# Two parts of a compression placed between the K/V groups of a sparse attention layer, and the turning of the Q rows beside the second part

## What is computed

```python
def nsa_shared_kv(s, w_kv, cmp_pe, cmp_w1, cmp_b1, cmp_w2, cmp_b2):
    kv = (s @ w_kv).reshape(B, S, 6, N_KV_HEADS, HEAD_DIM)
    k_c, v_c, k_s, v_s, k_w, v_w = kv[0], ..., kv[5]
    def compress(t, i):
        blocks = t[:, :, idx] + cmp_pe[i]              # 31 blocks of 32 tokens, stride 16
        flat = blocks.reshape(B, N_KV_HEADS, n_cmp, CMP_BLOCK * HEAD_DIM)
        hdn = jax.nn.gelu(flat @ cmp_w1[i] + cmp_b1[i])
        return hdn @ cmp_w2[i] + cmp_b2[i]
    kc = compress(k_c, 0)
    vc = compress(v_c, 1)
...
def nsa_mixer(u, ...):                                 # u = x * (1 + sc1) + sh1
    qg = u @ w_qg                                      # 1024 columns of Q, 48 of gates
```

## Time and profile before

| | |
|---|---|
| median of 3 runs | 1515.96 us (1513.84 to 1516.57) |
| the profiled execution | 1514.5 us, of which the span of the trace is 1512.7 us |
| PE busy | 1304.3 us (86%), mean granted clock 0.91 |
| DVE busy | 1077.6 us (71%) |
| ACT busy | 770.5 us (51%) |
| POOL busy | 304.5 us (20%) |

### The profile page before, as it was taken

One profiled execution on the slowest core, in us unless ns is written; L12 is line 12 of the kernel. 1 busy time (PEld: TensorE's weight loads), 2 busy tenths in 40 slices (PEclk: granted clock), 3 DMA queues, 4 the chain that ended last, 5 costly groups with the idle time before them and its releaser, 6 DMA issues.

```text
span 1512.7 us, 18392 instructions
## 1 busy us (share of the span) xinstructions
PE 1304.3 (86%) x6603; PEld 1013.3 (67%) x6603; DVE 1077.6 (71%) x1201; ACT 770.5 (51%) x998; POOL 304.5 (20%) x344
## 2 busy tenths in 40 slices
PE   1499988949999999869966899999984999999985
PEld 0277766847777777638964676775774777777772
DVE  5547773678888898565645566664276988988866
ACT  0323231327777777662422455657331777777760
POOL 3011111511000000107000445544441100000020
PEclk9699998759999999989957899999985999999998
DMA  8557765329999999924310333321531999999972
GB/s 311 217 186 243 266 223 225 119 84 367 391 388 382 393 392 386 375 97 143 114 55 6 112 98 99 112 79 62 198 135 54 367 405 389 391 387 390 392 289 91
DMA packets 107568, 356.07 MB, mean 235 GB/s; under 512 B 8034, under 2 KB 16446, under 8 KB 107470
## 3 DMA queue, kind: packets, MB, share of 16 engines
q1 hardware_dynamic: 82984, 269.52, 47.6%
q0 software_dynamic: 19952, 69.83, 13.3%
q10 hardware_dynamic: 4566, 15.84, 2.6%
HBM read 330.99 MB, written 25.21 MB: 235 GB/s over the span
## 4 chain that ended last, share of the span: by engine, by line
PE 51%; DVE 17%; issue 14%; ACT 9%; DMA 5%; POOL 2%; ACTq 1%; DVEq 0%; POOLq 0%; SPq 0%
PE bank L232 13%; PE bank L233 12%; PE bank L234 12%; ACT w_hi L1106 3%; DVE acc L360 3%; PE bank L1924 2%; PE bank L1942 2%; DMA xg<-scratch_u,tok 2%; PE bank L1912 1%; PE bank L1053 1%; DMA ada<-in_ada_w_dram 1%; DVE hh L1208 1%; POOL prob L2159 1%; PE bank L1147 1%; ACT xe_hi L1062 1%
## 5 line engine op out<-in xcount | busy, mean ns | idle before, releaser
L1112 DVE TENSOR_TENSOR w_lo<-raw,w_hi 128x2048 fp32r<-128x2048 f32 x189 | 436.9, 2317 | 69.8 <-ACT w_hi L1106 69.4
L1106 ACT ACTIVATE w_hi<-raw 128x2048 fp32r<-128x2048 f32 x189 | 362.5, 1919 | 84.6 <-PE bank L234 75.1
L232 PE MATMUL bank<-w_lo,xe_hi 128*128 128x512 f32 x512 | 211.9, 414 | 9.5 <-DVE xe_lo L1069 9.3
L234 PE MATMUL bank<-w_hi,xe_hi 128*128 128x512 f32 x512 | 203.9, 398 | 0.0
L233 PE MATMUL bank<-w_hi,xe_lo 128*128 128x512 f32 x512 | 203.6, 398 | 0.0
L227 DVE TENSOR_TENSOR w_lo<-raw,w_hi 128x2048 fp32r<-128x2048 f32 x37 | 85.7, 2321 | 144.8 <-ACT w_hi L222 144.7
L222 ACT ACTIVATE w_hi<-raw 128x2048 fp32r<-128x2048 f32 x37 | 70.5, 1909 | 160.0 <-PE bank L234 158.3
L232 PE MATMUL bank<-u_lo,w_hi 128*128 128x512 f32 x320 | 134.0, 419 | 17.8 <-DVE q L1826 9.3
L1042 POOL DMA_INDIRECT xg<-scratch_u,tok x32 | 38.2, 1194 | 551.2 <-DVE tok L1036 550.6
L233 PE MATMUL bank<-u_hi,w_lo 128*128 128x512 f32 x320 | 130.4, 407 | 0.0
L234 PE MATMUL bank<-u_hi,w_hi 128*128 128x512 f32 x320 | 130.3, 407 | 0.0
(11 more groups left out here) (289 smaller groups left out, 2378.5 us busy)
## 6 DMA issues: line engine op xcount, KB each, us to landing
raw<-in_w_gu_dram SPq DMA_DIRECT2D x128, 1024.0 KB, 8.2
raw<-in_w_down_dram SPq DMA_DIRECT2D x64, 1024.0 KB, 8.3
ada<-in_ada_w_dram POOLq DMA_DIRECT2D x64, 512.0 KB, 5.4
ada<-in_ada_w_dram SPq DMA_DIRECT2D x32, 512.0 KB, 3.8
scratch_y<-ye ACTq DMA_DIRECT2D x30, 512.0 KB, 7.5
raw<-in_conv_w_in_dram SPq DMA_DIRECT2D x12, 1024.0 KB, 9.7
raw<-in_w_kv_dram SPq DMA_DIRECT2D x6, 1024.0 KB, 8.4
rows<-scratch_mods POOLq DMA_DIRECT2D x10, 512.0 KB, 7.3
```

The source lines that it names most:

```text
L232: nc.tensor.matmul(o, lh, rl, start=start, stop=False)
L234: return nc.tensor.matmul(o, lh, rh, start=False, stop=stop)
L1106: nc.scalar.activation(w_hi[:, hslot, :], raw[:, slot, :], ACT.Copy).then_inc(hi_done, 1)
L1112: nc.vector.tensor_tensor(w_lo[:, slot, :], raw[:, slot, :], w_hi[:, hslot, :].bitcast(F32), ALU.subtract).then_inc(lo_done, 1)
```

## The change

The blocks are numbered in a new order, so that the two blocks of each part of the compression stand between K/V groups: group 0, group 1, part 0, group 2, part 1, Q. The loads, the splits and PE follow this order. The functions over all groups or both parts are cut into one per group or part, and the lists of `att_act` and `att_dve` are written out. PE turns the Q rows in four pieces: tile 0 and 1 before the first half of part 1, tile 2 and 3 between its halves. The first small product follows part 1, then the gates, then the second small product, then Q. The wait on `kc_made` moves behind the first half of the Q block. Group 2's K goes to banks 0 and 1, part 0 to banks 2 and 3, part 1 to banks 4 and 5, the turning to banks 2, 3, 6, 7. The buffers `w2`, `h1`, `kcf`, `vb2`, `wg` and `wg_hi` move from where the rows `u_hi` lie to the place of `kct`, which is free once `fl` is built; `wg_lo` takes the place of `wg`. POOL's small loads wait on `fl_made` and not on `blk_used`. No instruction of computation is added or left out.

```diff
+    B_KVG = [B_KV, B_KV + 2, B_KV + 6]
+    B_CMP = [B_KV + 4, B_KV + 8]
+    B_Q = B_KV + len(kv) + len(cmp1)
...
-        w2 = at("w2", [P, 2, HC, HD], F32, U0)
-        h1 = at("h1", [P, 2, HC, NC4], F32, U0 + KB)
-        kcf = at("kcf", [P, NC4], F32, U0 + 4 * KB)
-        wg = at("wg", [P, KD, 3 * NH], F32, S1 + 8 * KB)
+        w2 = at("w2", [P, 2, HC, HD], F32, S1)
+        h1 = at("h1", [P, 2, HC, NC4], F32, S1 + KB)
+        kcf = at("kcf", [P, NC4], F32, S1 + 3 * KB)
+        wg = at("wg", [P, KD, 3 * NH], F32, S1 + 4 * KB)
...
+        def compress_pe(pe, i, kh):
+            if kh == 0:
                 pe.wait_ge(fl_lo_made, i + 1)
                 if i == 0:
-                    pe.wait_ge(kv_v, 4)
-                    pe.wait_ge(kv_klo, 8)
...
+                    pe.wait_ge(kv_copy, 4)
+                else:
+                    pe.wait_ge(kv_v, 8)
...
+        def compress_out_pe(pe, i):
+
+            if i == 0:
+                pe.wait_ge(att_in, 16 * 3)
+                pe.wait_ge(*turn_q.lo.at(2 * TT))
+            pe.wait_ge(gelu_made, 2 * (i + 1))
...
         def q_pe(pe):
-            pe.wait_ge(kc_made, 3)
-            for i in range(TT):
-                turn_pe(pe, turn_q, us[:, i % 2, :], i)
...
+            pe.wait_ge(kv_klo, 8)
             for c_ in range(2):
                 if c_ == 1:
+                    pe.wait_ge(kc_made, 3)
...
         def att_pe(pe):
-            kv_pe(pe)
-            compress_pe(pe)
+            kv_pe(pe, 0)
+            kv_pe(pe, 1)
+            compress_pe(pe, 0, 0)
+            compress_pe(pe, 0, 1)
+            kv_pe(pe, 2)
+            pe.wait_ge(gelu_made, 2)
+            turn_pe(pe, turn_q, us[:, 0, :], 0)
+            pe.wait_ge(kv_v, 8)
+            turn_pe(pe, turn_q, us[:, 1, :], 1)
+            compress_pe(pe, 1, 0)
+            turn_pe(pe, turn_q, us[:, 0, :], 2)
+            turn_pe(pe, turn_q, us[:, 1, :], 3)
+            compress_pe(pe, 1, 1)
+            compress_out_pe(pe, 0)
+            gate_pe(pe)
+            compress_out_pe(pe, 1)
             q_pe(pe)
             attention_pe(pe)
...
-            pool.wait_ge(blk_used, B_CMP)
+            pool.wait_ge(fl_made, 1)
             pool.dma_start(w2[:], cmp_w2.rearrange("i (c p) d -> p i c d", p=P)).then_inc(att_in, 16)
...
-            pool.wait_ge(blk_used, B_Q)
+            pool.wait_ge(fl_made, 2)
             pool.dma_start(wg[:], w_qg[0].rearrange("(k p) n -> p k n", p=P)[:, :, D:D + 3 * NH]).then_inc(wg_in, 16)
...
         def att_sp(sp):
-            for b in range(3, 6):
-                load_block(sp, B_KV + b, kv[b])
+            load_block(sp, B_KVG[1] + 1, kv[3])
+            for kh in range(2):
+                load_block(sp, B_CMP[0] + kh, cmp1[kh])
...
```

More of the change, by code:

```diff
@@ L1578, in hybrid_trunk @@
         x_saved = sem("x_saved")
[L1580 to L1591, removed]
+        kbanks, vbanks = {1: (4, 5), 2: (0, 1)}, {1: (6, 7, 0, 1), 2: (4, 5, 6, 7)}
@@ L1600, in kv_pe @@
-                    if g:
-                        for i in range(TT):
[L1602 to L1669, removed]
@@ new lines, in kv_pe, with kct_act @@
+                            t = slice(i * P, (i + 1) * P)
+                            mm = mm3(bank[vbanks[g][i]][:, 0:2 * P], u_hi[:, k, t], u_lo[:, k, t],
+                                     wh[:, kk, 2 * P:4 * P], wl[:, kk, 2 * P:4 * P], start=(k == 0),
+                                     stop=(k == KD - 1))
+                        if kh == 1 and i < TT - 1:
+                            mm.then_inc(kv_mm, 1)
+                mm.then_inc(blk_used, 1)
+        def kct_act(act):
+            for m in range(4):
+                if m < 3:
+                    act.wait_ge(kv_mm, m + 1)
+                else:
+                    act.wait_ge(blk_used, B_KVG[0] + 2)
+                nc.scalar.activation(kct[:, m, :], bank[m][:], ACT.Copy).then_inc(kv_copy, 1)
@@ new lines, in k_hi_act @@
+        def k_hi_act(act, g):
+            for m in range(2):
+                act.wait_ge(kv_mm, 3 + 5 * (g - 1) + m + 1)
+                src = bank[kbanks[g][m]]
+                for h in range(2):
+                    part = slice(h * HD, (h + 1) * HD)
+                    for o in range(2):
+                        a = nc.scalar.activation(k2[o * HD:(o + 1) * HD, 2 * m + h, g - 1, :],
+                                                 src[part, :], ACT.Copy)
+                    a.then_inc(kv_khi, 1)
@@ L1699, in flat_lo_dve, with cmp_bank @@
             nc.vector.tensor_tensor(fl_lo[:], fl[:], fl_hi[:].bitcast(F32), ALU.subtract).then_inc(fl_lo_made, 1)
-        def compress_pe(pe):
-            for i in range(2):
+        def cmp_bank(i, hc):
+            return bank[(2, 4)[i] + hc]
+        def compress_pe(pe, i, kh):
+            if kh == 0:
                 pe.wait_ge(fl_lo_made, i + 1)
                 if i == 0:
-                    pe.wait_ge(kv_v, 4)
-                    pe.wait_ge(kv_klo, 8)
[L1707 to L1723, removed]
@@ new lines, in compress_pe @@
+                    pe.wait_ge(kv_copy, 4)
+                else:
+                    pe.wait_ge(kv_v, 8)
+            b = B_CMP[i] + kh
+            pe.wait_ge(lo_done, b + 1)
+            wh = w_hi[:, b % NSPLIT, :].rearrange("p (k n) -> p k n", n=HC * P)
+            wl = w_lo[:, b % NRAW, :].rearrange("p (k n) -> p k n", n=HC * P)
+            for kk in range(8):
+                k = 8 * kh + kk
+                for hc in range(HC):
+                    c_ = slice(hc * P, (hc + 1) * P)
+                    mm = mm3(cmp_bank(i, hc)[:, 0:NC4], wh[:, kk, c_], wl[:, kk, c_], fl_hi[:, k, :],
+                             fl_lo[:, k, :], start=(k == 0), stop=(k == 15))
@@ L1733, in compress_pe @@
[L1733 to L1744 removed]
+            mm.then_inc(kc_mm, 1)
```

189 lines of the change are left out of this document (134 added, 55 removed).

## The result

The changed kernel takes 1481.76 us (median of 4 runs, 1479.24 to 1484.10), the kernel before 1516.23 in the same session (4 runs, 1513.84 to 1516.57). The ratio is 0.9779, 95% interval [0.9759, 0.9798]: 34.5 us less. The forecast was 1486.

A forecast was written before the change was run, and what follows sets the result against it. A PE-DVE chain with the clock level on top bounds the stage before attention. The steps start attention at 809.0, not 838.5: 1514.5 less 29.5 is 1485.0, plus 1.5 to the median, stated as 1486; range 1478 to 1497.

The forecast's parts named there:

- the rival at 1481: Clock around part 1 not lost, or back at once; DVE then bounds tile 3; gain 34.7 us, chance 0.25.
- tile 1: PE turns the second tile of Q behind its wait for the V copies: 1.7 us.
- part 1, first half: 48 matmuls behind tile 1, taken at the low clock level: 10.3 us, against 5.3 at full clock.
- part 1, second half: Behind the transposes of tiles 2 and 3, taken at full clock: 5.3 us.
- small products: Behind part 1 on PE: 2.4 us, between half of the earlier 3.03 busy and all of it.
- The wait: PE stands 4.7 us behind tile 0, until DVE's list from part 0's end reaches group 2's last V copy.
- The clock: The 4.7 us wait loses the level; part 1's first half runs low, tiles 2 and 3 restore it for the second.
- The cover of the first `fl`: Beside POOL, `fl` and POOL's steps stretch 4 to 5 us at worst; `fl_lo` at 718, wanted at 727.3: 9 us.
- The gate weights: POOL's load issued at 746.8, landing in 3.4 us; ACT asks at about 751.2, so just in time.
- rival 4: ACT stands at late gate weights, delaying `k2`, V and tile 1; 1520 us and more, chance 0.02.
- Rivals 2 and 3: Low clock through both halves of part 1, 1493, chance 0.17; gain partly lost behind attention's start, about 1500, chance 0.07.
- the stage of before: From group 1's end on PE, put at 727.3, to the attention's first matmul at 838.46: 111.2 us.

The follow-up runs named there:

- e1: Against the kernel before: only both parts placed between the K/V groups, all Q tiles still turned behind part 1 and its small products; 1493.28 us.
- e2: Against the kernel before: only the Q rows turned beside part 1, with group 2 still ahead of both parts; 1488.26 us.
- e3: Changed kernel with 36 extra transposes on PE, results overwritten, ahead of tile 0 while PE waits for the V copies; 1489.13 us.
- e6: Changed kernel with 36 extra transposes ahead of tile 0 and DVE's w_lo of Q's first block moved behind u_lo of tile 1; 1483.44 us.
- e7: Changed kernel with only DVE's w_lo of Q's first block moved behind u_lo of tile 1; 1483.46 us.
- e4: Changed kernel with part 1 in banks 2 and 3, directly behind group 2, tiles turned in pairs behind each of its halves; 1478.86 us.
- e5: e4 with DVE's w_lo of Q's first block moved behind u_lo of all four tiles, kcf ahead of the two other splits; 1474.49 us.
- r3: e5 run again on a third chip, beside the changed kernel; 1477.81 us.

## Why the prediction was right

The time lies 4.2 us below the forecast, inside the range, and the mechanism is the forecast's, not that of the rival at 1481, though the number is near it: the clock was lost. That the time came out near 1481 has other sources, listed last.

| step (us) | predicted | measured |
|---|---|---|
| part 0 | 10.7 | 10.7 |
| group 2 | 22.3 | 22.6 |
| tile 0 | 1.2 | 1.0 |
| PE stands for the V copies | 4.7 | 4.5 |
| tile 1 | 1.7 | 0.9 |
| part 1, first half | 10.3 | 10.3 |
| tiles 2 and 3 | 3.4 | 3.3 |
| part 1, second half | 5.3 | 5.5 |
| small products | 2.4 | 1.6 |
| gates | 5.6 | 5.6 |
| from there to the attention | 14.1 | 14.2 |
| sum | 81.7 | 80.2 |

- **The wait.** DVE's list from part 0's end to the last V copy, 28.0 us in the prediction (27.6 of them added up from single rows), took 28.0 (27.8). That put the wait within 0.2 us.
- **The clock.** The prediction says: "work of this shape holds the level that it finds, while transposes in a row bring the high one back." In e1, with 0.56 us of idle ahead, 96 matmuls kept 1.00; here 48 stayed at 0.50 until tiles 2 and 3, and e2 repeats it. e3, where the idle was filled and only then the first half ran fast, shows that the wait is the cause. Which property of these matmuls keeps the low level low no run separates. The sentence needs one limit: in e3 the level fell while these matmuls were running, so a level found at their start is not yet safe behind a wait. The rule cited from the Trainium skill (TensorE: Matmul & The Clock Gate, What's actually happening), that sustained matmul activity releases the slow clock, would have had the first half fast early in its 10.3 us; in these traces it was not. The steps that erred are tile 1 and the small products, 0.8 us each: I priced tile 1 at a mixed level, but the level fell only at 763.8, when tile 1 was nearly done, and the small products ran high and took 1.6 us, where the prediction took 2.4, between half of 3.03 and all of it.
- **The cover of the first `fl`.** It took 13.16 us beside POOL, 4.7 more than the 8.4 alone, the worst case of 4 to 5 us. The price was not spread over it: two of its 16 additions took 2.67 and 2.58 us, each beside one step of POOL, 13 took 0.56 to 0.60, the first 0.93. POOL's steps there took 2.63 and 2.50 us against 2.40, so they hardly stretched. DVE, then POOL:

```profile
697.67 2.67 DVE L1674 TENSOR_TENSOR fl<-kct,small 64x248 f32<-64x248 f32 x1
700.36 2.58 DVE L1674 TENSOR_TENSOR fl<-kct,small 64x248 f32<-64x248 f32 x1
```
```profile
697.34 2.63 POOL L521 TENSOR_TENSOR xt<-xt,rows 128x1024 f32<-128x1024 f32 x1
700.05 2.50 POOL L523 TENSOR_TENSOR xt<-xt,rows 128x1024 f32<-128x1024 f32 x1
```

  `fl_lo` was made at 714.4, not 718, and PE asked at 724.2: 9.8 us of cover, 9 predicted.
- **The gate weights.** ACT and POOL by time:

```profile
744.15 0.90 POOL L2261 DMA_DIRECT2D wg<-in_w_qg_dram  x1 [30.36 <-DVE fl L1674]
```
```profile
746.41 1.92 ACT L223 ACTIVATE w_hi<-raw 128x2048 fp32r<-128x2048 f32 x1 [0.65 <-PE bank L235]
748.23 0.51 ACT L1820 ACTIVATE wg_hi<-wg 128x384 fp32r<-128x384 f32 x1
```

  Issued at 744.15, landed after 3.3 us, used at 748.23 with no idle ahead of it: "just in time" held, and rival 4 did not occur.
- **Rivals 2 and 3.** The second half ran at 0.11 us a matmul, so the level came back as forecast. The rest grew by 1.3 us, not by up to 13.6. (A longer rest was among the signs of being wrong; 1.3 us is less than two traces of one program differ by, 1.8.)
- **What the sum lacked.** Of the 4.2 us, 1.5 are the terms above, and 0.2 is the stage of before, read too short. Another 2.9 lie ahead of the stage, less 1.3 behind it: these are no merit of the change, and the forecast had neither. The last 0.9 is the 1.5 us that I put between the profiled execution and the median, less the rounding to 1486; in the result the two differ by 0.02. I called the part ahead unchanged; its instructions are, its time was not. Scatter would do: the changed kernel's three traces have group 1's end at 724.0 to 724.4, but the nine traces of the seven other kernels, which begin alike, have it at 723.8 to 727.9, and before, at 727.1, lies among them. With one trace of before this stays open.

## What to carry to other kernels

When a reordering lets one engine run ahead, add up the other engine's whole list in that place: the new wait is its backlog, and here single rows gave it within 0.2 us. Price a wait on PE at its length plus what the clock level costs behind it (4.5 us and 4.8 us here), and, as far as these traces show, place dense transposes where the level must return. A faster stage exposes the next wait, and a wait of 2 us beside small tiles cost a whole half of part 1 its level (e3); taking away both causes (banks and one split) gave 71.5 us of stage where either alone gave 75 and 80. Judge such a step by the time of the whole kernel as well: e6 has a stage 4 us shorter than e7's and the same median.

## What the runs showed of the hardware

- The granted clock fell behind short waits between small pieces of work: at 776.6 us in e3, behind one of 2.05 us that PE had already left; at 777.2 in e6, behind 0.88 us; at 775.2 in e4, with waits of 1.18 and 1.78. In e5 and in r3 one of 1.78 us alone did not lower it. The length of a wait alone doesn't tell it.
- In the changed kernel the fall at 763.8 came 0.8 us after PE had begun again (762.99). A trace that shows the low level first on busy matmuls can have its cause in the idle time ahead. At the attention's start the gap is longer still: in e1 PE is busy without a hole from 816.23, behind a wait of 0.73 us, and the level fell at 818.6.
- Of DVE's 16 additions with two inputs in SBUF, the two that met an addition of POOL (128x1024) took 2.67 and 2.58 us in place of 0.58, about as long as the step (2.63 and 2.50, against 2.40 without DVE): nearly all of the price was on DVE, while at 680 us both engines paid.
